# A gate round's convolution two chunks later, its LRU gates and attention scores exchanged, and the GLA norm's root of the last round beside the LRU's root

## The reference

```python
for l in range(DEPTH):                               # DEPTH = 2
    z = rms_norm(x, norm_g[l]) @ w_in[l]
    y_s5  = rms_norm(s5_mixer(...), s5_out_g[l])   * silu(s5_gate)
    y_mla = rms_norm(mla_mixer(...), mla_out_g[l]) * silu(mla_gate)
    y_gla = gla_mixer(...)                         * silu(gla_gate)   # rms-normed per head inside
    y_lru = rms_norm(rglru_mixer(...), lru_out_g[l]) * silu(lru_gate)
    x = x + concatenate([y_s5, y_mla, y_gla, y_lru]) @ w_out[l]
return rms_norm(x, final_g)

def rglru_mixer(x, ...):
    xc = causal_depthwise_conv(x, width=4) + conv_b          # per channel
    r = sigmoid(block_matmul(xc, w_a) + b_a)                 # 8 blocks of 128 channels
    i = sigmoid(block_matmul(xc, w_x) + b_x)
    log_a = -8 * r * softplus(-lam)
    return linear_scan(exp(log_a), sqrt(-expm1(2 * log_a)) * (i * xc))
```

## Time and profile before

| | |
|---|---|
| median of 3 runs | 2826.83 us (2826.18 to 2830.11) |
| the profiled execution's own time | 2828.15 us |
| its span in the trace | 2826.1 us, so 2.05 us lie around it |
| PE matmul busy | 2748.5 us (97%) |
| PE weight load busy | 2357.5 us (83%) |
| DVE busy | 2067.6 us (73%) |
| ACT busy | 1598.3 us (57%) |
| POOL busy | 783.3 us (28%) |
| mean DMA rate | 191 GB/s |
| granted TensorE clock, mean | 0.994 |

### The profile page before, as it was taken

How to read it: one execution, slowest core, us unless ns; L and a number is a source line. 1 busy time by engine, 2 the same in 40 slices (tenths; PEclk the granted TensorE clock), 3 DMA queues, 4 the chain that set the end, 5 groups by cost and what they waited for, 6 DMA issues and landing times.

```text
span 2826.1 us, 56434 instructions
## 1 busy us (share of the span) xinstructions
PE 2748.5 (97%) x15960; PEld 2357.5 (83%) x15960; DVE 2067.6 (73%) x3372; ACT 1598.3 (57%) x2872; POOL 783.3 (28%) x823
## 2 busy tenths in 40 slices
PE   6999999999999999999999999999999999999997
PEld 4888888888888888888878888888888888888886
DVE  8899899866666676555578999997666666855555
ACT  5555555656656575444455555556655656744443
POOL 3255555400110122111134555552010111411111
PEclk9999999999999999999999999999999999999998
DMA  6766666685655657777646565666755555577775
GB/s 217 254 189 175 182 179 187 169 264 168 186 167 167 185 145 218 209 211 209 205 145 209 176 186 175 187 177 189 244 185 165 169 182 165 168 215 212 208 210 176
DMA packets 294196, 538.88 MB, mean 191 GB/s; under 512 B 32432, under 2 KB 43584, under 8 KB 293056
## 3 DMA queue, kind: packets, MB, share of 16 engines
q1 hardware_dynamic: 268736, 497.45, 59.3%
q10 hardware_dynamic: 25344, 39.99, 4.3%
HBM read 516.34 MB, written 25.17 MB: 192 GB/s over the span
## 4 chain that ended last, share of the span: by engine, by line
PE 42%; DVE 3%; issue 3%; ACT 1%; POOL 1%; DVEq 0%; ACTq 0%; POOLq 0%
PE ps L323 26%; PE ps L322 13%; DVE w L1049 1%; PE ps L325 0%; DVE zb L1618 0%; DVE yy L1118 0%; ACT w L626 0%; PE ps L354 0%; DVE g L1112 0%; PE ps L365 0%; POOL lg L1672 0%; ACT half_lo L632 0%; PE ps L342 0%; PE ps L502 0%; PE ps L501 0%
## 5 line engine op out<-in xcount | busy, mean ns | idle before, releaser
L323 PE MATMUL ps<-hb,w 128*128 128x512 f32 x5824 | 2053.1, 396 | 7.4 <-POOL hb L1648 6.1
L1049 DVE TENSOR_TENSOR w<-raw,w 128x512 fp32r<-128x512 f32 x1828 | 1340.2, 743 | 637.9 <-ACT w L626 628.8
L626 ACT ACTIVATE w<-raw 128x512 fp32r<-128x512 f32 x1828 | 1131.2, 629 | 946.6 <-PE ps L323 935.5
L322 PE MATMUL ps<-hb,w 128*128 128x256 f32 x5690 | 1619.4, 285 | 19.7 <-DVE w L1049 18.2
L323 PEld LDWEIGHTS ps<-hb,w 128*128 128x128 f32 x5824 | 1090.9, 188 | 255.9 <-issue 6.7
L322 PEld LDWEIGHTS ps<-hb,w 128*128 128x128 f32 x5690 | 1074.4, 189 | 62.3 <-DVE w L1049 36.1
L323 PE MATMUL ps<-gl,w 128*128 128x512 f32 x800 | 283.5, 395 | 0.0
L1810 POOL TENSOR_TENSOR nf<-zb 128x256 f32 (+1 forms) x60 | 51.9, 865 | 537.2 <-DVE zb L1586 531.6
L322 PE MATMUL ps<-gl,w 128*128 128x256 f32 x680 | 190.3, 280 | 0.0
L323 PE MATMUL ps<-w,hb 128*128 128x512 f32 x512 | 180.7, 396 | 0.0
L323 PEld LDWEIGHTS ps<-gl,w 128*128 128x128 f32 x800 | 149.5, 188 | 30.2
(11 more groups left out here) (312 smaller groups left out, 2416.4 us busy)
## 6 DMA issues: line engine op xcount, KB each, us to landing
raw<-in_w SPq DMA_DIRECT2D x1843, 256.0 KB, 2.8
hd<-heads ACTq DMA_DIRECT2D x16, 512.0 KB, 5.4
gate<-xres ACTq DMA_DIRECT2D x32, 256.0 KB, 4.3
xres<-zb ACTq DMA_DIRECT2D x32, 256.0 KB, 3.6
zb<-in_x SPq DMA_DIRECT2D x8, 512.0 KB, 7.2
xres<-in_x SPq DMA_DIRECT2D x4, 1024.0 KB, 6.6
s5w<-in_s5w ACTq DMA_DIRECT2D x16, 256.0 KB, 3.5
out<-zb SPq DMA_DIRECT2D x4, 1024.0 KB, 3.9
```

The lines of the kernel that those rows point to most:

```text
L322: mm(acc[:, T:], a_lo, m_hi, start=False, stop=False, skip_group_check=True)
L323: last = mm(acc, a_hi, m_both, start=(k == 0), stop=(k == nk - 1), skip_group_check=True)
L626: A(w2[:, d, :, 0, :], raw[:, s, :, :], ACT.Copy).then_inc(hi_ready, count)
L1049: V.tensor_tensor(w2[:, d, :, 1, :], raw[:, s, :, :], w2[:, d, :, 0, :].bitcast(F), ALU.subtract).then_inc(w2_ready, count)
```

## The change

The order of instructions within a gate round changes; apart from one thing, no operation is added or removed. The one thing is in the last round of each layer: GLA's root needs no activation table of its own any more, and the preload that followed it is dropped. The core of the diff:

```diff
-Y_LAST = {5: 0, 8: 1, 11: 2, 14: 3, 21: 4, 22: 5}
+Y_LAST = {5: 0, 8: 1, 11: 2, 16: 3, 21: 4, 22: 5}
...
                     def gla_columns():
                         pe.wait_ge(yg_squared, l * G8 + 6)
                         pe.wait_ge(st_ready, it + 1)
-                        columns([(ssq[:, i, :],) for i in (2, 3, 4)], B_B)
+                        columns([(ssq[:, i, :],) for i in (2, 3, 4)], B_Y)
 
                     def gla_spread():
-                        pe.wait_ge(hf_ready, l * 32 + (16 + 1))
+                        pe.wait_ge(hf_ready, l * 32 + (16 + 3))
...
-                    steps = {5: [lru_gates], 6: [mla_scores], 9: [gla_gate],
+                    steps = {5: [mla_scores], 6: [lru_gates], 9: [gla_gate],
...
-                        steps[7] = [gla_spread]
+                        steps[13] = [gla_spread]
...
-                    steps = {0: [inputs], 5: [lru_tanh],
+                    steps = {2: [inputs], 6: [lru_tanh],
...
-                        A(ncol[:, 0:6], ps[:, B_B, 0:6], ACT.Sqrt, bias=EPS1, scale=1.0 / (BR // 4)).then_inc(rms_ready, 1)
+                        A(ncol[:, 0:6], ps[:, B_Y, 0:6], ACT.Sqrt, bias=EPS1, scale=1.0 / (BR // 4)).then_inc(rms_ready, 1)
 
                     if last:
-                        steps[1] = [gla_root, silu_set]
+                        steps[9] = [lru_root, gla_root]
...
-                    steps = {0: [lambda: conv(1), lambda: conv(2)], 1: [lambda: conv(3)], 
+                    steps = {2: [lambda: conv(1), lambda: conv(2)], 3: [lambda: conv(3)],
...
-                        steps[2] = [lambda: reciprocals(c_l + 4, 6)]
+                        steps[10] = [lambda: reciprocals(c_l + 4, 6)]
...
-                        if c == 0:
+                        if c == 2:
                             dve.wait_ge(pg_ready, it + 1)
-                        if last and c == 8:
+                        if last and c == 16:
                             dve.wait_ge(rstd_ready, c_l + 4)
```

## The result

The changed kernel takes 2810.80 us (median of 5 runs, 2809.54 to 2812.45), the kernel before 2827.01 beside it (median of 5, 2826.18 to 2830.11). The ratio is 0.9942, 95% interval 0.9931 to 0.9952. The profiled execution took 2810.80 and its span is 2808.8.

What follows compares the result with a forecast made beforehand. PE's matmuls fill 97% of the span, so only PE's waits can be won. Loop 10.3, last round's start 1.8 and middle 1.9 sum to 14.0 us: forecast 2812.8 us, own range 2811.5 to 2814.5.

Steps and rivals of the forecast that it cites:

- the loop's mechanism: Loop rounds: splits of chunks 4 and 5 go ahead of the convolution's wait, filling it; the wait itself doesn't move.
- Rivals 2 and 3: 2: wait partly returns at chunks 6 to 10, 2818.0 us, chance 0.09; 3: wait only moves, 2823 us, chance 0.05.
- rival 4: Gates in all 16 rounds: third tap slips past chunk 6, PE waits, slower at 2832 us; chance 0.03.
- I use idle + 0.15 for every such wait: PE's waits for DVE's low halves: each loses its printed idle plus 0.15 us, 0.87 for 0.71 idle.
- 12 x 0.86 = 10.3: Rounds 1 to 6 of both layers: convolution at chunk 2 removes 0.86 us a round, 10.3 us in all.
- 15 us: all waits gone: Low end of the forecast's own range, 2811.5 us: all waits gone, with one execution's noise.
- 1.8 + 1.9 = 3.7: Last rounds, both layers: 1.8 us from the wait at the start, 1.9 from two waits in the middle.
- 0.3 for the spread: Last round's middle: PE waits 0.1 to 0.4 us for part 2's product at the moved spread; 0.3 taken as cost.
- 0.1 for part 3: Last round's middle: part 3's splits meet DVE's `gla_qk` and chunks 21 and 22; cost taken as 0.1 us.
- rival 1: Last round: POOL's part 3 product meets DVE work, PE waits up to 1.35 us; 2815.6 us, chance 0.17.
- Exchange: zero: Gates and scores exchanged on PE: same matmuls in other order, gain zero, gates with 3.0 us spare.
- Round 0: nearly: Round 0: its 1.3 us wait for chunk 3 stays; gain 0, at most 0.1 us per layer at chunk 4.

Runs made afterwards that it cites:

- The run with one chunk: Changed kernel with the convolution one chunk later than in the kernel before, instead of two: 2812.35 us, ratio 0.9942.
- one tap: Kernel before with only the first convolution tap ahead of chunk 4's low half, the second and third behind it: 2823.30 us, ratio 0.9981.
- the last two: Changed kernel with round 0's chunk 3 split and SiLU table load earlier: 2809.47 us; the same with POOL's part 3 behind the squares: 2808.25 us.

## Why the prediction was right, and where it missed

**What bounds it, and the loop's mechanism: right.** The wait was filled and not moved: no wait in rounds 1 to 6, the convolution's start as far behind the last product as before, and the convolution alone gives all of it (0.98 a round with the place alone). Rivals 2 and 3 are refuted by the empty rows of the stretches, rival 4 by the gates: PE goes from chunk 5 into the scores `L501`, and from chunk 6 into the gates `L492`, with no idle time ahead of either.

```profile
735.86 0.38 PE L501 MATMUL ps<-hd 128*128 128x128 f32 x2
...
738.56 0.59 PE L492 MATMUL ps<-probt,mixw 128*128 128x256 f32 x2
```

**The step that failed: "I use idle + 0.15 for every such wait".** The 0.15 came from the start of the late matmul alone. The next one starts 0.11 late as well, and that was one row further in the trace of before. The price is the idle + 0.27, which the runs showed at idles of 0.71, 1.22 and 1.29 us, and at 0.19 with a second loss of 0.11 behind it. Of the mis-sized term, 12 x 0.86 = 10.3 should have been 12 x 0.98 = 11.8, that is 1.5 of the 2.2 us by which the forecast fell short. The low end of the range had the same fault: "15 us: all waits gone" was a bound made of waits priced too low, and the time fell below it. By the right price the same waits are 11.8 + 1.8 + 2.7 + 6 x 0.11 = 17.0.

**Last round: mechanism right, size 0.7 low in sum.** Forecast 1.8 + 1.9 = 3.7, measured 4.4. In layer 1, gone are 0.88, 0.81 and 0.52 of the three waits and 0.43 of the second starts behind them; also 0.22 at a start behind the transposes `L508`, in the kernel before 1024.29 to 1024.75, which the forecast did not see. New are the spread's 0.22 (0.12 at its start, the rest at its own pace) and 0.65 at `L526`. That is 1.99; of 2.15 some 0.16 stays spread over starts that no row names. The forecast's 0.3 for the spread and 0.1 for part 3 are 0.4 where 0.87 came; it was near only because the price of the waits was low too. The 0.1 was the wrong row: I had named the overlap of POOL's part 3 with `gla_qk` and the low halves as rival 1, but followed it only to the low halves of chunks 20 to 22, not to the evacuation behind them and the SiLU and `ym` that ACT makes from it.

**Exchange: zero, right,** by its own run. **Round 0: nearly.** The wait of 1.3 stands, as forecast, but the round is 0.18 shorter in each layer, where at most 0.1 was allowed for. In the kernel before, chunk 4 of round 0 was just late: its first matmul starts 0.33 behind the one ahead (631.04 to 631.37) instead of 0.23, and the second 0.22 behind the first, with no idle printed. Both are gone after the change. That is 0.36 us in all, outside the 16.2 above.

**Spare times.** Chunk 4 was to be ready 1.4 us before it is needed. It is ready at 732.33 (731.64 + 0.69), and PE wants it two chunks ahead of the scores, 735.86 - 2.80 = 733.06: 0.7 spare. DVE starts the two low halves 0.90 behind its last product where I had 0.2; the trace names ACT, but ACT's second high half had ended at 731.14. The run with one chunk has the same 0.90 at the same place, and its DVE timeline names another cause:

```profile
732.35 0.80 DVE L1049 TENSOR_TENSOR w<-raw,w 128x512 fp32r<-128x512 f32 x1 [0.90 <-DVEq L252]
```

`L252` belongs to `own.restart()`, with which DVE ends each loop round: it raises its own counter, waits for it and clears it. That this is all of the 0.90 no run isolates. It cost PE nothing. The sentence on `L932` "still 1.2 us behind the end of the old round's last product" was a slip: the rows of before give 0.71, and it is 0.71 after.

**The rule on the shared port.** The Trainium skill, SBUF — State Buffer, "SBUF: two separate sides", lets a DVE instruction with two SBUF inputs and a GpSimd one that reads SBUF exclude each other for a whole instruction. The trace agrees: DVE's three take 1.39, 0.83 and 1.22 us and end 0.54, 0.28 and 0.54 behind the ends of POOL's three (1019.39, 1020.41, 1021.29), and they take 0.68, 0.41 and 0.68 when POOL's part 3 is moved off. The forecast counted it for the low halves and the copies, and left out that what it delays is all that stands behind on DVE.

## What to carry to other kernels

Before pricing a wait from the idle time in a view, read the start of the two instructions behind it against an undisturbed place of the same pattern, and price by the distance of a repeated landmark; here 0.11 of each 0.98 stood in the second row. Ask for the view of the weight loads too: it prints waits that the matmuls' view leaves out (next section). Fill a wait by moving work that is ready ahead of it, as far as the consumer's lead lets you and no further than needed: one chunk did it as well as two. Where two engines share a port, follow a lengthened instruction to everything queued behind it, evacuations and the engine that reads them included, and not only to the kind of instruction that was late before.

## What the runs showed of the hardware that was not expected

After a wait of PE the second matmul starts 0.22 us behind the first instead of 0.12, whatever the wait's length (0.19, 0.71 and 1.22 us of idle), and a chunk that is only just in time shows it with no idle printed (736.85 to 737.07 above). The timeline of the weight loads (PEld) shows what changes. First the kernel before, ahead of the wait and behind it, then the chunk with one tap that is just in time:

```profile
734.73 0.19 PEld L322 LDWEIGHTS ps<-hb,w 128*128 128x128 f32 x1
734.96 0.19 PEld L323 LDWEIGHTS ps<-hb,w 128*128 128x128 f32 x1
736.17 0.19 PEld L322 LDWEIGHTS ps<-hb,w 128*128 128x128 f32 x1 [1.02 <-DVE w L1049]
736.28 0.19 PEld L323 LDWEIGHTS ps<-hb,w 128*128 128x128 f32 x1
```

```profile
736.85 0.19 PEld L322 LDWEIGHTS ps<-hb,w 128*128 128x128 f32 x1 [0.16 <-DVE w L1049]
```

Undisturbed, the weights of a first matmul are loaded from 0.23 us ahead of its start (734.73 for 734.96), and those of the second from the first's start on. Behind the wait the first load starts with its own matmul (736.17 and 736.18), the second load 0.11 later, and the second matmul 0.12 behind its load, as ahead of the wait. So it is the load that waits for DVE's low half, and the second pair is late because its load stands behind one that was not made ahead. In this view the chunk that is just in time does have a wait. Measured against its normal place, the start of the `L323` matmul ahead of it, the first load is 0.23, 0.57, 1.09 and 1.61 us late in the four cases (the just-timely chunk, then idles of 0.19, 0.71 and 1.22), and PE loses 0.11, 0.46, 0.98 and 1.49: each time 0.11 to 0.12 less. What inside the engine sets that difference is not shown.

The layers' first part, which none of the edits but the last two comes near, differs between executions: PE's waits for DVE's `w` from 60 to 420 us, in the profiles of the kernel before, the changed kernel, and the changed kernel again:

```profile
PE ps L322 <- DVE w L1049: 2.8, 6, 0.8
```

```profile
PE ps L322 <- DVE w L1049: 1.9, 4, 0.8
```

```profile
PE ps L322 <- DVE w L1049: 2.7, 7, 0.8
```

The last two are the same code. So a difference of about 1 us between two profiled spans says nothing of a change here; the landmarks inside the changed rounds do.
